# Moving the experts' row numbers and first row loads into the end of the router

## What is computed

```
h = rmsnorm(x, moe_norm)
g_sel = argmax(h @ router_group)                  # 1 of 4 groups
top_p, top_i = top_k(softmax(h @ router_expert[g_sel]), 2)   # 2 of 8 experts
expert = g_sel * 8 + top_i
y = sum over the two: gate * (silu(h @ w1[e]) * (h @ w3[e])) @ w2[e]
x = x + y
```

## Time and profile before

| | us |
|---|---|
| median of 3 runs (1823.37 to 1824.29) | 1823.58 |
| profiled execution, its time | 1821.84 |
| profiled execution, its span | 1820.1 |
| TensorE busy, share of the span | 1656.2, 91% |
| VectorE busy | 1167.3, 64% |
| ScalarE busy | 489.8, 27% |
| DMA, mean over the span | 259 GB/s |

### The profile page before, as it was taken

How to read it: one execution, slowest core, us unless ns; L and a number is a source line. 1 busy time by engine, 2 the same in 40 slices (tenths; PEclk the granted TensorE clock), 3 DMA queues, 4 the chain that set the end, 5 groups by cost and what they waited for, 6 DMA issues and landing times. The chain is left out here.

```text
span 1820.1 us, 27622 instructions
## 1 busy us (share of the span) xinstructions
PE 1656.2 (91%) x10944; PEld 888.5 (49%) x11073; DVE 1167.3 (64%) x1926; ACT 489.8 (27%) x854; POOL 181.1 (10%) x234
## 2 busy tenths in 40 slices
PE   6999989989969999999997999889779999999995
PEld 4666677855533333333332779654433333333332
DVE  5467877783337677777777533693427776777766
ACT  5253334453301111111112411573211111111112
POOL 2000734411100000000000000351100000000000
PEclk9999999999979999999998999999989999999997
DMA  5541000024769999999995220206669999999993
GB/s 159 154 134 35 6 3 4 3 94 165 292 262 406 425 425 424 426 424 424 425 424 222 88 93 24 93 2 258 272 244 426 425 424 425 425 426 424 424 421 132
DMA packets 101474, 471.46 MB, mean 259 GB/s; under 512 B 29152, under 2 KB 68064, under 8 KB 75744
## 3 DMA queue, kind: packets, MB, share of 16 engines
q1 hardware_dynamic: 99040, 461.26, 63.1%
q0 software_dynamic: 2304, 8.39, 1.1%
HBM read 452.85 MB, written 16.78 MB: 258 GB/s over the span
## 5 line engine op out<-in xcount | busy, mean ns | idle before, releaser
L681 PE MATMUL ps<-w_unit,xT 128*48 128x512 f32 x1024 | 451.7, 594 | 6.1 <-issue 4.6
L682 PE MATMUL ps<-w_unit,xT 128*48 128x512 f32 x1024 | 451.7, 594 | 0.0
L783 DVE SCALAR_TENSOR_TENSOR x<-ps,gate_by_expert,x 128x512 f32<-128x512 f32 x512 | 348.4, 744 | 137.3 <-PE ps L733 137.2
L681 PEld LDWEIGHTS ps<-w_unit,xT 128*48 128x48 f32 x1024 | 125.9, 123 | 311.0 <-issue 309.0
L711 PE MATMUL ps<-w_unit,hidT 128*48 128x512 f32 x1024 | 248.4, 605 | 12.1 <-issue 12.1
L806 ACT ACTIVATE y_high_low<-y_cut 48x512 fp32r<-48x512 f32 x128 | 80.4, 628 | 402.2 <-DVE y_cut L754 399.7
L733 PE MATMUL ps<-y_high_low,slots_to_tokens 128*128 128x512 f32 x512 | 158.1, 430 | 14.4 <-DVE y_high_low L758 13.2
L733 PEld LDWEIGHTS ps<-y_high_low,slots_to_tokens 128*128 128x128 f32 x512 | 88.0, 192 | 131.9 <-issue 66.1
L1245 PE MATMUL ps<-hT_high,w_high 128*128 128x512 f32 (+1 forms) x344 | 139.7, 406 | 10.0 <-PE ps L1247 3.7
L1247 PE MATMUL ps<-hT_high,w_low 128*128 128x512 f32 (+1 forms) x344 | 135.9, 395 | 0.0
L1246 PE MATMUL ps<-hT_low,w_high 128*128 128x512 f32 (+1 forms) x344 | 135.5, 394 | 0.0
(11 more groups left out here) (368 smaller groups left out, 2232.6 us busy)
## 6 DMA issues: line engine op xcount, KB each, us to landing
w_unit<-in_moe_w SPq DMA_DIRECT2D x184, 2048.0 KB, 27.4
w_unit<-in_moe_w SPq DMA_DIRECT2D x16, 1024.0 KB, 33.4
x_rows<-sorted_rows SPq DMA_DIRECT2D x64, 192.0 KB, 26.9
w_unit<-in_od_w_qkv SPq DMA_DIRECT2D x12, 1024.0 KB, 5.3
w_raw<-in_ev_w_in SPq DMA_DIRECT2D x10, 1024.0 KB, 6.9
sorted_rows<-bias SPq DMA_DIRECT2D x32, 192.0 KB, 5.6
w_unit<-in_ev_w_out SPq DMA_DIRECT2D x2, 2048.0 KB, 11.6
w_unit<-in_od_w_out SPq DMA_DIRECT2D x2, 2048.0 KB, 11.6
```

The lines of the kernel that those rows point to most:

```text
L681: nc.tensor.matmul(ps_1[0:MB, :], xT[b][:, k, :], w1[:, k, :], start=k == 0, stop=k == KD - 1)
L682: last = nc.tensor.matmul(ps_3[UP:UP + MB, :], xT[b][:, k, :], w3[:, k, :], start=k == 0, stop=k == KD - 1)
L783: nc.vector.scalar_tensor_tensor(out=xs, in0=ps_c[i % 4][:, :], scalar=gate(t), in1=xs, op0=ALU.mult, op1=ALU.add).then_inc(added, 1)
```

## The change

The row numbers' part moves from the start of `experts` to the end of `router`: after the last count matmul TensorE runs 24 of the small matmuls, the two sums of diagonals and 40 more; VectorE makes the diagonals directly after the last `destine` and copies the result between gates and tables. POOL makes the slots' numbers at the router's start. The gain is loaded once. `xn` holds two tiles that take turns, so the squares of tiles 2 and 3 wait for the scatters of tiles 0 and 1. SP waits for all scatters, loads the rows of the first three experts in the router, and issues piece 9 behind them.

```diff
@@ Routes @@
+        self.row_of = c.sb("row_of_token", [P, 2, T], mybir.dt.int16, ctx=ctx, side="right")
...
+        self.x_rows = [c.sb(f"x_rows{j}", [P, XG, P], ctx=ctx, side="right") for j in range(SLOTS)]
+        self.rows_in = [c.lasting_sem(f"rows_in{j}") for j in range(SLOTS)]
@@ router, SP @@
             sp.wait_ge(out_done, 2 * TT)
-            wts.load(sp, GUEST)
+            wts.load(sp, GUEST[:1])
+            for j in range(2):
+                sp.wait_ge(scattered[j], 16 * TT)
+            for n in range(SLOTS):
+                r.load_rows(sp, xrows, n, n * CAP)
+            wts.load(sp, GUEST[1:])
@@ router, TensorE @@
+            keep_warm(nc, c, ps_idle, 24)
+            for j in range(2):
+                pe.wait_ge(diag_made, j + 1)
+                nc.tensor.matmul(ps_row[j][:, :], c.ones[:, :], yT[:, j, :], start=True, stop=True).then_inc(row_done, 1)
+            keep_warm(nc, c, ps_idle, 40)
@@ router, ScalarE, for tile i @@
+                if i >= 2:
+                    act.wait_ge(scattered[i % 2], 32 * (i // 2))
-                nc.scalar.activation(xn[:, t, :], x[:, t, :], ACT.Square,
+                nc.scalar.activation(xn[:, i % 2, :], x[:, t, :], ACT.Square,
@@ router, VectorE @@
             destine(LAST)
+            dve.wait_ge(dest_done, TT)
+            for j in range(2):
+                V.tensor_tensor(yT[:, j, :].rearrange("p (t n) -> p t n", t=TT),
+                                c.ident[:, :].rearrange("p (o n) -> p o n", o=1).to_broadcast([P, TT, P]),
+                                row[:, :, j:j + 1].to_broadcast([P, TT, P]), ALU.mult).then_inc(diag_made, 1)
...
+            for j in range(2):
+                dve.wait_ge(row_done, j + 1)
+                V.tensor_copy(r.row_of[:, j, :], ps_row[j][:, :])
             dve.wait_ge(pos_done, TT + 1)
@@ router, POOL (the same lines go from experts) @@
+            made = chain(pool, slots_made)
+            for ap, step in ((r.slot_row[:, :], CAP), (r.slot0[:, :], 0)):
...
-                        in_=xn[:, t, :], in_offset=None).then_inc(scattered, 16)
-            pool.wait_ge(scattered, 16 * 2 * TT)
+                        in_=xn[:, i % 2, :], in_offset=None).then_inc(scattered[i % 2], 16)
+            for j in range(2):
+                pool.wait_ge(scattered[j], 16 * TT)
@@ experts, SP @@
-            for n in range(SLOTS):
-                load_rows(sp, slot(n), n * CAP)
-                if n == 0:
-                    sp.dma_start(g[:, :], gain_dram.rearrange("(p k) -> p k", k=KD)).then_inc(gain_in, 16)
             wts.load(sp, range(GUEST[-1] + 1, UNITS))
@@ experts, TensorE @@
-            keep_warm(nc, c, ps_y[0], 40)
-            for j in range(2):
-                pe.wait_ge(diag_made, j + 1)
-                nc.tensor.matmul(ps_c[j][:, :], c.ones[:, :], (cut, acts)[j][:, :],
-                                 start=True, stop=True).then_inc(row_done, 1)
-            pe.wait_ge(gain_in, 16)
             turn_rows(pe, 0, 0)
@@ experts, VectorE @@
-            for j, tile in enumerate((cut, acts)):
-                V.tensor_tensor(tile[:, :].rearrange("p (t n) -> p t n", t=TT),
...
-            dve.wait_ge(slots_made, 8)
-            dve.wait_ge(gain_in, 16)
             gain_rows(dve, 0, 0)
-            for j in range(2):
-                dve.wait_ge(row_done, j + 1)
-                V.tensor_copy(row_of[:, j, :], ps_c[j][:, :]).then_inc(row_out, 1)
-            dve.wait_ge(row_out, 2)
-            dve.sem_inc(row_out, 1)
             gain_rows(dve, 1, 1)
@@ experts, ScalarE @@
-            act.wait_ge(row_done, 2)
             silu(act, 0)
```

More of the change, by code:

```diff
@@ L283, in router @@
     wr = c.sb("w_router", [P, KD, NL], ctx=ctx)
-    g = c.sb("gain", [P, KD], ctx=ctx)
+    g = r.gain
     ss = c.sb("ss", [P, 2, TT], ctx=ctx)
@@ L314, in router @@
                                                                      "dest_done"))
-    sub_done, exp_done, own, scattered = c.sem("sub_done"), c.sem("exp_done"), c.sem("dve_own"), c.sem("scattered")
+    sub_done, exp_done, own = c.sem("sub_done"), c.sem("exp_done"), c.sem("dve_own")
+    scattered = [c.sem(f"scattered{j}") for j in range(2)]
+    slots_made, diag_made, row_done = c.sem("slots_made"), c.sem("diag_made"), c.sem("row_done")
     c.of_stage += wts.guest_in
     ps_out, ps_turn, ps_lg, ps_pos = ps[0:4], ps[4:6], ps[6], ps[7]
-    ps_count = ps_out[0]
+    ps_count, ps_row, ps_idle = ps_out[0], ps_out[1:3], ps_out[3]
     HALF = KD // 2
@@ L416, in _ @@
                 act.wait_ge(rstd_done, i + 1)
-                nc.scalar.activation(xn[:, t, :].rearrange("p (k q) -> p k q", k=KD),
+                nc.scalar.activation(xn[:, i % 2, :].rearrange("p (k q) -> p k q", k=KD),
                                      x[:, t, :].rearrange("p (q k) -> p k q", k=KD), ACT.Copy,
@@ L525, in _ @@
         def _(pool):
+            made = chain(pool, slots_made)
+            for ap, step in ((r.slot_row[:, :], CAP), (r.slot0[:, :], 0)):
+                for lo in (0, UP):
+                    p = slice(lo, lo + UP)
+                    made(nc.gpsimd.iota(ap[p, :], [[step, ap.shape[-1]]], base=0, channel_multiplier=1,
+                                        allow_small_or_imprecise_dtypes=True))
+                    made(nc.gpsimd.affine_select(out=ap[p, :], in_=ap[p, :], compare_op=ALU.is_ge, fill=NO_ROW,
+                                                 base=MB - 1, pattern=[[0, ap.shape[-1]]], channel_multiplier=-1))
             for i in range(TT):
@@ L621, in experts @@
 def experts(nc, c, ctx, ps, x, xrows, r, gain_dram, wts, ahead):
-    x_rows = [c.sb(f"x_rows{j}", [P, XG, P], ctx=ctx) for j in range(SLOTS)]
+    x_rows, g, row_of, slot_row, slot0, rows_in = r.x_rows, r.gain, r.row_of, r.slot_row, r.slot0, r.rows_in
+    c.of_stage += rows_in
     xT = [c.sb(f"xT{b}", [P, KD, MB], ctx=ctx) for b in range(2)]
@@ L634, in experts @@
     hidT = c.sb("hidT", [P, KF, MB], ctx=ctx)
-    g = c.sb("gain", [P, KD], ctx=ctx)
-    row_of = c.sb("row_of_token", [P, 2, T], mybir.dt.int16, ctx=ctx)
     cut = c.sb("y_cut", [P, FF], ctx=ctx)
@@ L640, in experts @@
     sel = [c.sb(f"slots_to_tokens{b}", [P, T], F32R, ctx=ctx) for b in range(2)]
-    slot_row, slot0 = c.sb("slot_row", [P, N_EXP], ctx=ctx), c.sb("first_slot", [P, 1], ctx=ctx)
     far = c.sb("further_slot", [P, 4], ctx=ctx)
@@ L646, in experts @@
     GROUPS = 2 * TT
-    gain_in = c.sem("gain_in")
-    rows_in = [c.sem(f"rows_in{j}") for j in range(SLOTS)]
     xT_done, xT_out = c.sem("xT_done"), c.sem("xT_out")
@@ L654, in experts @@
     compared, sel_made, spread_out, added = c.sem("compared"), c.sem("sel_made"), c.sem("y_spread"), c.sem("x_added")
-    slots_made, far_out = c.sem("slots_made"), c.sem("further_slot_out")
-    diag_made, row_done, row_out, own = c.sem("diag_made"), c.sem("row_done"), c.sem("row_out"), c.sem("dve_own")
+    far_out, own = c.sem("further_slot_out"), c.sem("dve_own")
     LAST, OWN = N_EXP - 1, 19
@@ L820, in further @@
         eng.nop()
-    def load_rows(sp, j, row):
-        rows = xrows[bass.ds(row, MB), :].rearrange("r (k n) -> (r k) n", k=KD).rearrange("(p i) n -> p (i n)", i=XG)
-        sp.dma_start(x_rows[j][:, :, :].rearrange("p i n -> p (i n)"), rows).then_inc(rows_in[j], 16)
     with nc.Block() as block:
[L828 to L837, removed]
         @block.sync
         def _(sp):
-            for n in range(SLOTS):
-                load_rows(sp, slot(n), n * CAP)
-                if n == 0:
-                    sp.dma_start(g[:, :], gain_dram.rearrange("(p k) -> p k", k=KD)).then_inc(gain_in, 16)
             wts.load(sp, range(GUEST[-1] + 1, UNITS))
@@ L853, in _ @@
                 sp.wait_ge(xT_done, n - SLOTS + 1)
-                load_rows(sp, slot(n), n * CAP)
+                r.load_rows(sp, xrows, slot(n), n * CAP)
                 if n in HALVED:
@@ L876, in more @@
                 sp.wait_ge(down_done, m + N_EXP)
-                load_rows(sp, XSLOT, row)
+                r.load_rows(sp, xrows, XSLOT, row)
                 for part in range(len(PARTS)):
@@ L936, in _ @@
             dve.sem_inc(low_out, 1)
-            for j, tile in enumerate((cut, acts)):
-                V.tensor_tensor(tile[:, :].rearrange("p (t n) -> p t n", t=TT),
-                                c.ident[:, :].rearrange("p (o n) -> p o n", o=1).to_broadcast([P, TT, P]),
-                                r.row[:, :, j:j + 1].to_broadcast([P, TT, P]), ALU.mult).then_inc(diag_made, 1)
             for h in range(2):
@@ L1034, in __init__ @@
         self.row = c.sb("row", [P, TT, 2], ctx=ctx, side="right")
+        self.row_of = c.sb("row_of_token", [P, 2, T], mybir.dt.int16, ctx=ctx, side="right")
+        self.slot_row = c.sb("slot_row", [P, N_EXP], ctx=ctx, side="right")
+        self.slot0 = c.sb("first_slot", [P, 1], ctx=ctx, side="right")
+        self.gain = c.sb("moe_gain", [P, KD], ctx=ctx, side="right")
```

(7 more changed lines are left out.)

## The result

| runs | before, median us | after, median us | ratio, 95% interval |
|---|---|---|---|
| first set (4 and 4) | 1823.47 | 1812.9 (1808.89 to 1813.86) | 0.9942 [0.9927, 0.9957] |
| second set (11 and 5), same kernels | 1822.66 | 1808.64 (1807.46 to 1812.89) | 0.9919 [0.9905, 0.9933] |

Both medians lie in the forecast range. The profiled execution after the change took 1813.25 us, its span 1811.5, which is 8.6 less than before.

The account below looks back on a forecast made before the run. TensorE bounds the experts, weights arriving 4.9 us early, so starting expert 0 earlier moves the stage. Per layer 7.0 - 2.5 + 1.28 = 5.8, twice, plus 1.75: 13.3 less, median 1810.3 us, range 1805.0 to 1817.0.

Parts of the forecast that it names:

- the table: ScalarE's table load for silu moves from behind expert 0's up to the stage's start: 1.28 us gained per layer.
- the dip: Layer 1's 3.5 us at low clock behind expert 0 vanish: 1.75 us gained once, bounds 0 and 1.75.
- expert 0's earlier start: At the router-experts seam, expert 0's matmuls begin at 517.7 in layer 0: 7.0 us earlier per layer.
- the low clock: TensorE begins expert 0 at the low clock for 5 us: 2.5 us lost per layer, bounds 0 and 4.05.
- the 516 that was named as a sign of being wrong: VectorE's last router step in layer 0, forecast at 514.65; one after 516 would show the prediction wrong.
- SP's list ... is done before VectorE ... VectorE is now the last engine: Router's end: SP's row loads and piece 9 add about 2 us, yet SP and POOL finish before VectorE.
- The stage change: From the router's last engine, taken as VectorE, to the experts' start: 1.0 us, upper bound 2.55.
- A: Rival: the clock stays up through the stage change; 18.3 us less in all, 1805.3; chance 0.10.
- D: Rival: the clock stays low far into the experts, costing 10.25 us per layer; 1827.5, slower; chance 0.04.
- B: Rival: router's end grows, both sums low and stage change 2.55 us; 8.2 less with the dip, 1815.4; chance 0.18.
- Costs at nothing: POOL's small steps, squares of tiles 2 and 3 waiting for scatters, and piece 9's later issue cost no time.
- Rival C: Piece 9's 4.9 us of traffic delays the weight loads, so TensorE waits at the end: 1823.6; chance 0.05.

Follow-up runs that it names:

- e4: Changed kernel with only expert 0's row load left in the router; the loads of experts 1 and 2 and piece 9 at the experts' start: 1810.12 us, one run.
- e1: Changed kernel with a second wait, on expert 0's transposes, ahead of layer-stage silu(0): 1808.5 us (4 runs), ratio 0.9926.
- e6: Changed kernel with 80 instead of 40 small zero matmuls behind the sums: 1805.88 us (6 runs), ratio 0.9912.
- e2: Kernel before the change without its wait for row_done ahead of silu(0): 1818.15 us (12 runs) against 1822.48, ratio 0.9972.
- e5: Changed kernel with the three row loads back at the experts' start and piece 9 directly behind piece 8; row numbers stay in the router: 1820.55 us, one run.
- e10: Changed kernel with diagonals made tile by tile, 80 zeros, and only expert 0's rows loaded in the router: 1805.96 us (6 runs), ratio 0.9911.
- e8: Changed kernel with the diagonals made tile by tile in destine, each behind its own dest step: 1811.97 us, one run.
- e9: Changed kernel with diagonals made tile by tile and 80 zeros: 1805.76 us (5 runs), ratio 0.9905.
- e3: Changed kernel with piece 9 issued beside piece 8 again, ahead of the scatters; rows still loaded in the router: 1818.44 us, one run.

## Why the prediction came out right

**The sum.** Forecast 5.8 + 5.8 + 1.75 = 13.3 us; the trace gives 6.35 + 5.33 + 1.19 = 12.9 at the same places. The two sets of runs give 10.6 and 14.0, around it. That the sum came so close is in part luck: the table (0.4 too much in each layer) and the dip (0.6 too much) were put too high, expert 0's earlier start (0.6 over both layers) and the low clock (0.2 in each layer) the other way.

**Expert 0 starts 7.0 earlier:** 7.83 and 6.73. Two errors offset each other. VectorE's list ended 8.3 to 8.7 us behind the mark instead of 9.3, since the pair of sums began 0.3 sooner and took 2.24 / 2.65 and not 2.9. (Its last step lies at 516.29 in layer 0, past the 516 that was named as a sign of being wrong; but the whole execution runs 2.6 us later there, and by the mark the step is early.) And the step "SP's list ... is done before VectorE ... VectorE is now the last engine" was wrong: the scatters landed 4.2 to 5.2 us after their issue instead of 4.0, POOL's first issue was 0.43 longer, and SP ended 0.36 / 0.95 us behind VectorE. e4 shows for layer 1 that this held the stage, by 0.8 us. It is close: in e1's layer 0, with the same list, VectorE ended 0.2 behind SP. The stage change itself, from SP's end to the first instruction, was 1.1 us (1.0 forecast; in e4, from VectorE's end, 1.2); from there to the first weight matmul 1.7 us (2.0).

**Low clock at expert 0, 2.5:** 2.3, shown by e6. Expert 0 began low and rose at about 524, as forecast; rivals A and D did not come. Nor did B in full: its stage change of 2.55 us was 1.1, and its sums of 3.9 were 2.24 / 2.65. The Trainium skill (TensorE: Matmul & The Clock Gate, HAM oscillation) has it that idle gaps between groups of matmuls cost each group a slow start. The trace agrees: 0.50 behind the 3.4 us gap ahead of the transposes at 517.84, 1.00 in e6, where the zeros fill it.

**Silu's table, 1.28:** 0.86 per layer in e1 and e2. The mechanism was right, its size not. With the load gone, `hidden` (530.03) no longer follows silu (over at 529.53) directly; it follows the gain of expert 1 (529.44 + 0.56), which VectorE has ahead of it. The other 0.42 us went to this next wait. The page of the Trainium skill that was weighed (ScalarE: Activation LUTs, What ACT_TABLE_LOAD costs) adds a drain to the load; the trace differs: in e1 the load ends at 524.21 and the operation starts at 524.23.

**Layer 1's dip, 1.75:** 1.19, the shortening of layer 1's experts behind expert 1's start. The forecast took half of the 3.5 us as lost; the twelve traces have 1.2 for such a stretch, and why it isn't half is not shown. e1 brought the dip back and e2 took it out of the kernel before, so it goes with the long wait for silu. The wait alone does not decide it: of the four layers with 2.83 or 2.84 us (before and e1) both layers 1 have the dip and neither layer 0; of the twenty with 1.96 or 1.97 none has.

**Costs at nothing** held. Timeline of ScalarE, layer 0, after; it answers to the earlier trace rows:
```profile
484.92 1.06 ACT L422 ACTIVATE xn<-x 128x1024 f32<-128x1024 f32 x1 [8.71 <-DMA sorted_rows<-xn,dest]
489.60 0.60 ACT L425 ACTIVATE yT<-ps 128x512 f32<-128x512 f32 x1 [3.53 <-PE ps L370]
498.98 1.06 ACT L422 ACTIVATE xn<-x 128x1024 f32<-128x1024 f32 x1 [5.91 <-DVE x L447]
```
Tile 2's square did wait for a scatter, and ScalarE was idle for 3.53 us behind it all the same; tile 3's waited for its addition alone. Rival C fell too. TensorE's waits in layer 1's experts, after (us in total, times, longest), name no weight load:
```profile
PE ps L759 <- DVE y_high_low L784: 6.6, 2, 3.3
PE ps L737 <- issue: 6.1, 13, 0.5
PE ps L707 <- DVE xT L764: 1.4, 1, 1.4
```

**What stays open.** The two sets differ by the clock: of the changed kernel's nine runs the four with a mean granted clock of 0.968 or 0.969 took 1812.6 to 1813.9 us, the five with 0.971 to 0.973 took 1807.5 to 1809.5. Three of the first set's four runs are of the former kind, and one of the second's five. Both traces are of the former too, so where the other five save some 5 us is not seen in one of them. e1's trace, at 0.973, reaches the first router 5.8 us sooner than the changed kernel's first trace and takes 1.1 less in layer 0's experts behind expert 1's start. The first router starts at 434.31 and 433.71 in the changed kernel's two traces and at 431.15 before. With e1, whose code up to there is the changed kernel's, it starts at 428.50, so the late start is not forced by the change; with e2 it starts at 428.76. These two have the least low clock ahead of it, 24 us; the others, with 27 to 41 us, lie between 431.2 and 435.0, though not in the order of these lengths (34 us with e5 at 434.97, 41 with e10 at 432.26). That the change makes such executions likelier is not excluded by one or two traces per kernel.

## What to carry to other kernels

A seam between stages ends with whichever list is last, so when work moves into the end of a stage, add up every list from the slowest DMA landing on, SP's issues behind it too: here SP, and behind it the rows' landing, was last by less than a microsecond, and in some executions VectorE was. Fill TensorE's idle time up to the change of stage itself, not up to the last real matmul: 40 more zeros gave 2.3 us per layer and cost some 0.15. Where runs of one kernel differ by 5 us, marks inside the trace can decide a question of 1 us that medians can't, once several traces of the same code have shown how far each mark moves by itself.

## What was not expected of the hardware

POOL's issue of a scatter took 1.39 us in both layers while VectorE multiplied two 512-column tiles at the same time (508.17 to 509.46), and 0.96 without that, in e8, e9 and e10 too, which still run the zeros beside it: so it goes with these long products. The Trainium skill (SBUF — State Buffer, SBUF: two separate sides) says that VectorE, when it reads two SBUF inputs, and a GpSimd operation that reads SBUF lock each other out of a shared port pair for an instruction's length. The 0.43 us fits into the 0.55 for which the products still ran once the issue had begun; no run here shows that the port pair is the reason.

A 2 MB load issued ahead of the scatters' end delayed their landing by 2.7 and 2.3 us by the medians: 7.2 and 7.4 in e3, 4.5 and 5.1 after the change. It holds in every trace: tile 3's scatters land after 6.4 to 7.8 us in both layers of the four kernels with piece 9 early (before, e2, e3, e5), and after 3.4 to 5.4 in the other eight.

The same code met different low-clock stretches in different executions: 24 to 41 us of them ahead of the first router in twelve traces, with the router's start between 428.5 and 435.0.
